# x loaded first on two queues, and the table set of Ln and Exp loaded by hand ahead of each norm's sum

## The reference

```python
def rms_norm(x, w):
    y = x * lax.rsqrt(jnp.mean(x * x, axis=-1, keepdims=True) + EPS)
    return y * w

for i in range(2):
    hn = rms_norm(h, norm_mix_pre[i])
    m = deltanet_stickbreak_mixer(hn, ...) if i == 0 else s5_mixer(hn, ...)
    h = h + rms_norm(m, norm_mix_post[i])
    hn = rms_norm(h, norm_ffn_pre[i])
    h = h + rms_norm(swiglu_ffn(hn, ...), norm_ffn_post[i])
```

## Time and profile before

| | us |
|---|---|
| median of 3 runs | 3101.07 (3097.99 to 3101.18) |
| profiled execution | 3102.59 |
| its span | 3100.8 |
| PE busy | 2824.9 (91%) |
| ACT busy | 684.9 (22%) |
| DVE busy | 1235.6 (40%) |
| GpSimd busy | 948.7 (31%) |

### The profile page before, as it was taken

The page is one execution under the profiler, slowest core; times in us unless marked ns, Lnnn a source line. Parts: engine busy times, 40 slices in busy tenths (PEclk is TensorE's granted clock), DMA queues, the critical chain, the costliest instruction groups (busy, mean ns, idle before and its releaser), DMA issues.

```text
span 3100.8 us, 44315 instructions
## 1 busy us (share of the span) xinstructions
PE 2824.9 (91%) x17789; PEld 2701.1 (87%) x17789; DVE 1235.6 (40%) x2076; ACT 684.9 (22%) x1168; POOL 948.7 (31%) x390
## 2 busy tenths in 40 slices
PE   3999979989999999999999876559999999999996
PEld 2999968877888999999999775459989999999995
DVE  2665137755424444444433421630152233222234
ACT  3222125545434000000001431220250000000012
POOL 3344400000043443443333322005243444443330
PEclk8999989999999999999999987679999999999998
DMA  4222441111122222222221235961122111111102
GB/s 136 70 89 96 109 90 38 42 49 42 45 80 76 70 94 70 70 76 76 70 86 63 87 67 138 212 161 55 47 96 78 48 50 51 41 50 44 41 28 73
DMA packets 171849, 232.67 MB, mean 75 GB/s; under 512 B 58464, under 2 KB 137312, under 8 KB 169440
## 3 DMA queue, kind: packets, MB, share of 16 engines
q1 hardware_dynamic: 66064, 133.42, 15.0%
q10 hardware_dynamic: 105680, 97.77, 10.2%
HBM read 171.12 MB, written 60.03 MB: 75 GB/s over the span
## 4 chain that ended last, share of the span: by engine, by line
issue 35%; PE 32%; POOL 13%; DVE 7%; DMA 7%; ACT 4%; ACTq 2%; SPq 1%; POOLq 0%; DVEq 0%
POOL w_hi L600 8%; PE psum L628 6%; PE psum L629 6%; PE psum L630 6%; POOL w_lo L604 4%; DMA stage<-wstream 4%; PE psum L686 3%; DVE area L1944 2%; PE psum L1036 2%; PE psum L1008 1%; PE psum L887 1%; PE psum L877 1%; DVE area L1866 1%; DVE area L1871 1%; DMA area<-s_u 1%
## 5 line engine op out<-in xcount | busy, mean ns | idle before, releaser
L628 PE MATMUL psum<-x_hi,w_hi 128*128 128x344 f32 (+2 forms) x3600 | 1165.9, 324 | 55.2 <-DVE x_lo L1889 26.9
L629 PE MATMUL psum<-x_lo,w_hi 128*128 128x344 f32 (+2 forms) x3600 | 1159.1, 322 | 0.0
L630 PE MATMUL psum<-x_hi,w_lo 128*128 128x344 f32 (+2 forms) x3600 | 1154.2, 321 | 0.0
L600 POOL TENSOR_TENSOR w_hi<-stage,const 128x1024 fp32r<-128x1024 f32 x193 | 470.2, 2436 | 2047.0 <-PE psum L630 2027.3
L628 PEld LDWEIGHTS psum<-x_hi,w_hi 128*128 128x128 f32 x3600 | 681.4, 189 | 63.3 <-DVE x_lo L1889 26.6
L629 PEld LDWEIGHTS psum<-x_lo,w_hi 128*128 128x128 f32 x3600 | 680.6, 189 | 1.9
L630 PEld LDWEIGHTS psum<-x_hi,w_lo 128*128 128x128 f32 x3600 | 681.4, 189 | 0.0
L604 POOL TENSOR_TENSOR w_lo<-stage,w_hi 128x1024 fp32r<-128x1024 f32 x193 | 482.7, 2501 | 15.1
L628 PE MATMUL psum<-act_hi,w_hi 128*128 128x344 f32 (+1 forms) x1056 | 347.4, 329 | 22.1 <-DVE area L2331 16.7
L630 PE MATMUL psum<-act_hi,w_lo 128*128 128x344 f32 (+1 forms) x1056 | 342.0, 324 | 0.0
L629 PE MATMUL psum<-act_lo,w_hi 128*128 128x344 f32 (+1 forms) x1056 | 341.0, 323 | 0.0
(11 more groups left out here) (214 smaller groups left out, 2293.5 us busy)
## 6 DMA issues: line engine op xcount, KB each, us to landing
stage<-wstream SPq DMA_DIRECT2D x193, 512.0 KB, 3.6
s_set<-area ACTq DMA_DIRECT2D x8, 1860.0 KB, 7.9
proj<-area ACTq DMA_DIRECT2D x28, 520.0 KB, 2.6
area<-proj ACTq DMA_DIRECT2D x36, 256.0 KB, 3.5
resid<-area ACTq DMA_DIRECT2D x6, 1376.0 KB, 6.0
area<-resid ACTq DMA_DIRECT2D x6, 1376.0 KB, 9.8
area<-proj ACTq DMA_DIRECT2D x12, 520.0 KB, 5.0
area<-xT ACTq DMA_DIRECT2D x4, 1376.0 KB, 8.1
```

Source lines behind the costliest of these rows:

```text
L600: pool.tensor_tensor(per_block(w_hi[:, slot, :]), per_block(stage[:, h, :]), all_ones, ALU.mult).then_inc(high_split, 1)
L628: mm(out[:, 0:n], w_hi[:, slot, wk], hi[:, xk, a:a + n], start=first, stop=False)
L629: mm(out[:, 0:n], w_hi[:, slot, wk], lo[:, xk, a:a + n], start=False, stop=False)
L630: return mm(out[:, 0:n], w_lo[:, slot, wk], hi[:, xk, a:a + n], start=False, stop=last)
```

## The change

Stage 0 gets a buffer for part 2 of x (`first_h`), a second set of buffers for squares and a second bank for the sum of part 1. ACT issues part 0 of x first of all; SP issues the first 256 columns of `const`, `small`, parts 1 and 2, then the rest of `const`, all ahead of the weights. The zero writes move behind the convolution loop. In stage 0 part 1's squares no longer wait for part 0's sum, and PE's second sum waits for nothing but them. DVE's memsets of `rows`, `ga` and `gb` move ahead of stage 0, and its order there becomes pre 0, pre 1, low 0, pre 2, low 1, low 2. Every `norm_root` begins with a load of the set `natural_log_exp_and_others`, ahead of its wait for the sum, and so does the gates' part.

```diff
@@ norm buffers @@
+        first_h = [nv["h"][0], nv["h"][1], carve(3 * T_ROWS, KT, 344)]
+        first_sq = [sq_halves, [carve(3 * T_ROWS + KT * 344, 4, 344), carve(A1 + 3 * KT * CW, 4, 344)], sq_halves]
+        first_sums = [bank[7], bank[6], bank[7]]
@@ SP @@
+            sp.dma_start(const[:, 0:2 * P], const_in[:, 0:2 * P]).then_inc(params_loaded, 16)
+            sp.dma_start(small[:], small_in).then_inc(params_loaded, 16)
+            for c in (1, 2):
+                a, n = CUTS[c]
+                sp.dma_start(first_h[c][:, :, 0:n], xT[:, :, a:a + n]).then_inc(first_loaded[c], 16)
+            sp.dma_start(const[:, 2 * P:N_CONST_USED], const_in[:, 2 * P:N_CONST_USED]).then_inc(zeros_written, 16)
@@ PE norm_sum @@
-                if r == 0 and c:
-                    pe.wait_ge(nm_normed, c)
+                if r == 0:
+                    if c == 2:
+                        pe.wait_ge(nm_normed, 1)
@@ ACT norm_square @@
-                if e:
+                if r == 0 and c == 2:
+                    act.wait_ge(nm_sum, 1)
+                elif r:
                     act.wait_ge(nm_sum, e)
@@ ACT norm_root @@
+                nc.scalar.preload_act_table_set("natural_log_exp_and_others")
                 act.wait_ge(nm_sum, e + 1)
@@ ACT opening @@
-            act.dma_start(small[:], small_in).then_inc(params_loaded, 16)
-            act.dma_start(const[:], const_in[:, 0:N_CONST_USED]).then_inc(params_loaded, 16)
+            norm_load(0, 0)
             act.wait_ge(eps_ready, 3)
-            zeros = carve(18300, FRONT)
-            for g in range(4):
-                act.dma_start(proj[4 * g:4 * g + 4, :, 0:FRONT].rearrange("m p t -> p m t"),
...
-            act.dma_start(s5_k.rearrange("c m g w -> c (m g) w")[:, :, CH * G_CH:LAGS * G_CH],
...
-            act.wait_ge(params_loaded, 32)
-            norm_load(0, 0)
-            norm_load(0, 1)
             norm_square(0, 0, 1)
+            norm_square(0, 1, 1)
             norm_root(0, 0, 1)
-            norm_square(0, 1, 1)
+            norm_square(0, 2, 1)
             norm_root(0, 1, 1)
             norm_high(0, 0)
-            norm_load(0, 2)
             norm_high(0, 1)
-            norm_square(0, 2, 1)
             norm_root(0, 2, 1)
             norm_high(0, 2)
...
+            nc.scalar.preload_act_table_set("natural_log_exp_and_others")
             act.wait_ge(nm_normed, 3)
             ch(A(gate_col[0:4, :], small[0:4, A_LOG:A_LOG + 1], ACT.Exp))
...
             with act.Fori(0, 3) as i:
                 conv_tiles(i)
+            zeros = carve(18300, FRONT)
+            for g in range(4):
+                act.dma_start(proj[4 * g:4 * g + 4, :, 0:FRONT].rearrange("m p t -> p m t"),
...
+            act.dma_start(s5_k.rearrange("c m g w -> c (m g) w")[:, :, CH * G_CH:LAGS * G_CH],
...
             act.wait_ge(s5["params"], 16)
...
-            act.wait_ge(zeros_written, 80)
+            act.wait_ge(zeros_written, 96)
@@ DVE opening @@
-            dve.wait_ge(params_loaded, 32)
-            for c in range(3):
-                norm_pre(0, c)
-                norm_low(0, c)
...
             ch(V.memset(rows, 0.0))
             ch(V.memset(ga, 0.0))
+            ch.sync()
+            V.memset(gb, 0.0).then_inc(gate_dve, 1)
+            dve.wait_ge(params_loaded, 32)
+            norm_pre(0, 0)
+            norm_pre(0, 1)
+            norm_low(0, 0)
+            norm_pre(0, 2)
+            norm_low(0, 1)
+            norm_low(0, 2)
...
+            dve.wait_ge(x_ready, 3)
             ch(V.memset(keep, 1.0))
...
-            V.memset(gb, 0.0).then_inc(gate_dve, 1)
             dve.wait_ge(gate_act, 1)
```

More of the change, by code:

```diff
@@ L449, in trunk @@
         norm_sums = bank[7]
+        first_h = [nv["h"][0], nv["h"][1], carve(3 * T_ROWS, KT, 344)]
+        halves_of = lambda x: [x[:, 4 * i:4 * i + 4] for i in range(2)]
+        sq_halves = halves_of(nv["sq"])
+        first_sq = [sq_halves, [carve(3 * T_ROWS + KT * 344, 4, 344), carve(A1 + 3 * KT * CW, 4, 344)], sq_halves]
+        first_sums = [bank[7], bank[6], bank[7]]
         DOWN_BANKS = 3
@@ L675, in norm_sum @@
                 e = norm_event(r, c, m)
-                if r == 0 and c:
-                    pe.wait_ge(nm_normed, c)
+                sums, sq = (first_sums[c], first_sq[c]) if r == 0 else (norm_sums, sq_halves)
+                if r == 0:
+                    if c == 2:
+                        pe.wait_ge(nm_normed, 1)
                 elif r == 4 and c:
@@ L685, in norm_sum @@
                         pe.wait_ge(nm_square, 2 * e + k // 4 + 1)
-                    last = mm(norm_sums[:, 0:n], ones, nv["sq"][:, k, 0:n], start=(k == 0), stop=(k == KT - 1))
+                    last = mm(sums[:, 0:n], ones, sq[k // 4][:, k % 4, 0:n], start=(k == 0), stop=(k == KT - 1))
                 last.then_inc(nm_sum, 1)
@@ L1189, in norm_square @@
                     ks = slice(4 * half, 4 * half + 4)
-                    A(nv["sq"][:, ks, 0:n], x[:, ks], ACT.Square).then_inc(nm_square, 1)
+                    A(sq[half][:, :, 0:n], x[:, ks], ACT.Square).then_inc(nm_square, 1)
             def norm_root(r, c, m):
@@ L1214, in norm_high @@
                 act.wait_ge(nm_normed, 3 * r + c + 1)
[L1215 to L1218 removed]
+                h = first_h[c] if r == 0 else nv["h"][c % 2]
+                A(x_hi[:, :, a:a + n], h[:, :, 0:n], ACT.Copy).then_inc(nm_high, 1)
+            norm_load(0, 0)
             act.wait_ge(eps_ready, 3)
[L1221 to L1229 removed]
             for _i in range(6):
@@ L1309, in _ @@
                 conv_tiles(i)
+            zeros = carve(18300, FRONT)
+            for g in range(4):
+                act.dma_start(proj[4 * g:4 * g + 4, :, 0:FRONT].rearrange("m p t -> p m t"),
+                              zeros.rearrange("p (a t) -> p a t", a=1).to_broadcast([P, 4, FRONT])
+                              ).then_inc(zeros_written, 16)
+            no_lag = (LAGS - CH) * G_CH
+            act.dma_start(s5_k.rearrange("c m g w -> c (m g) w")[:, :, CH * G_CH:LAGS * G_CH],
+                          zeros[0:G_CH, 0:no_lag].rearrange("p (a t) -> p a t", a=1).to_broadcast([G_CH, KT * GPT, no_lag])
+                          ).then_inc(zeros_written, 16)
             act.wait_ge(s5["params"], 16)
@@ L1888, in norm_low @@
                 dve.wait_ge(nm_high, 3 * r + c + 1)
-                V.tensor_tensor(x_lo[:, :, a:a + n], nv["h"][c % 2][:, :, 0:n], x_hi[:, :, a:a + n].bitcast(F32), sub
+                h = first_h[c] if r == 0 else nv["h"][c % 2]
+                V.tensor_tensor(x_lo[:, :, a:a + n], h[:, :, 0:n], x_hi[:, :, a:a + n].bitcast(F32), sub
                                 ).then_inc(x_ready, 1)
```

20 lines of the change are left out of this document (11 added, 9 removed).

## The result

The changed kernel takes 3050.71 us (3045.43 to 3054.22) against 3101.12 in the same comparison; the ratio is 0.9837, with a 95% interval from 0.9818 to 0.9855. That is 50.4 us less, where 43.4 were forecast; the time lies in the range of 3047 to 3067.

What follows compares the result with a forecast made beforehand. TensorE, busy 91% of a 3100.8 us span, bounds the kernel, so only its idle places can be won: 33 (opening) + 0.4 (convolutions) + 10 (norm loads) = 43.4, giving 3057.7 us, range 3047 to 3067.

Steps and rivals of the forecast that it cites:

- The load of x: Opening: first part of x lands at 11.5 (bounds 9.5 and 15.6), including some 3 us of start and receipt.
- The gates: Six gate groups at 2.8 us each, starting at 35.6; projection starts at 55.4 against 88.70, gain 33.
- The term of 2 us: Gates: 2 us added once for a low clock after PE idles, before the first two groups.
- The rival with the low clock: Zero writes cost 7.7 and PE is at 1.2 GHz after each opening pause, 2 + 3.7 dearer: 3063.4; chance 0.10.
- The chain behind the gates: From gates to first convolution: 4.4 us shorter relative to PE, by the early memset (3.1) and a dropped table load.
- The convolutions: Convolution stage: they bound PE; PE's time moves by the zero writes' price less 4.4, taken -0.4.
- Z: Price of the zero writes moved behind the last convolution tile: taken as 4, with 7.66 and 2.8 as alternatives.
- The hand-loaded set: Later norms: Exp's 1.28 us load saved where PE idles for the result; sum 10.0, bounds 7 and 14.
- The delta-net rows: Evidence that one set serves Ln and Exp: there Exp follows Ln with no load and no idle time.
- the rival that the hand load does nothing: Ln and Exp keep getting own loads; the 10 and some 3 in the opening are lost: 3070.7; chance 0.04.
- upper bound of 14, for two places: Later norms' gain is 14 if a shorter idle keeps the clock up at two of the places.
- Drain: Rival: every load costs the drain too, 2.66 us a switch; eight times 1.38 more, 3046.7; chance 0.03.

Runs made afterwards that it cites:

- e8: The changed kernel with all three parts of x on SP's queue, ACT's queue empty in the opening; 3054.83 us.
- e7: The changed kernel with DVE's memset of gb, and the signal letting ACT read the gates, back behind the other memsets; 3048.15 us.
- e10: e3 with GpSimd's second split operation cut to 64 of 1024 columns for 24 of the projection's 28 slabs, computation partly left out; 3037.61 us.
- e9: e5 plus four matmuls of constants between the gates and the projection; 3037.74 us, ratio 0.9800.
- e11: e3 plus four matmuls of constants ahead of the projection; 3039.23 us, ratio 0.9799.
- e1: The changed kernel without its hand-made table loads, the opening staying as changed; 3082.52 us, ratio 0.9923.
- e2: The kernel before with one edit, the table set loaded at the head of every norm root; 3078.28 us, ratio 0.9923.
- e5: The changed kernel with the gates in three products of 352, 344 and 344 columns in place of six of half that; 3050.39 us.
- e3: The changed kernel with matmuls of constants in PE's two idle times: 8 before the first gate group, 9 before the third; 3054.28 us.

## Why the prediction was right, and where it was not

The sign and the total held: 50.4 us by medians, 54.3 between the spans, for 43.4. That the total came so close is luck: the gain up to the projection was 7 us too high, and the convolutions and the later norms brought 9 and 8 more than forecast. Step by step:

**The load of x.** Forecast 11.5 for the first square, with bounds of 9.5 and 15.6; it came at 8.98, below the lower bound. The 3 us for start and receipt stand in no row and were too many. Nor did SP's traffic beside it cost what the sum took: in e8, with no other part of x beside it, the first part gained only 0.6. That the queues bring nothing held (e8); the reading of 214 GB/s as what one queue moves did not, since one queue moved 350 to 364 there. What the buffer for the third part, the second set of squares and DVE's new order brought each was not tried alone. PE's wait of 15.8 us for the third part's squares, ahead of the sum at 63.30 in the kernel before, is gone as well. GpSimd's splits started at 19.18 as forecast (19), and DVE's `x_lo` beside them took 3.90 and then 5.0 each, as taken (5.27).

**The gates.** This is the step that failed. The sum took six groups at 2.8 us and 2 us for a low clock, and had 19.8 us from the first gate matmul to the projection; it was 30.4, at 1.2 GHz but for the first 0.9. The term of 2 us came from a sum's products: seven of them ran at 0.50 in 4.1 us before the clock came back (this window is the second sum's, 344 columns, though the 7.16 set beside it is the first's; the second took 7.06). It was carried over to products of half the width, with which the clock did not come back. Mis-sized by some 11 us; with the gates' start 3.8 us early, that makes 26.4 of the forecast 33. The early start is in part the first square's 2.5, and `x_ready` 2 came at 41.7 and not at the 44 that was taken (44.9 by the walk's own durations). The rival with the low clock carried it as 2 more.

**The chain behind the gates.** ACT did follow PE through the gates and was through with Ln 4.3 us behind PE in place of 8.2, so 3.9 sooner, where 4.4 were forecast. But the DVE part of that chain (16.1 us from 66.66 to 82.71) was 3.3 longer than before, since some of its operations met GpSimd's split, and the lead over PE at the first convolution was 0.6 and not 4.4. e7 shows that the memset itself was worth nothing.

**The convolutions.** The forecast let PE's waits shrink by the lead less the zero writes' 4 us. In fact the stretch fell by 9.4: the chain went over from 1940 to 1620 ns an operation, left PE behind, and the zero writes then fell into slack. The forecast had treated DVE's times as fixed, though rows 5 had shown such an operation at 5.27 in place of 3.09 beside GpSimd. The mechanism is shown by e10 and by the meetings counted in all traces: six fewer, at 1.9 us each, make up the 11.5 us by which the 36 operations got shorter. That moving the two groups against each other changes the course is shown by e9 and e11. The change was not made for that, so this gain is luck. Why 8.21 us still gave the fast course and 8.81 the slow one was not tested, and that e1's fastest execution had the fast course is a guess from its time.

**The zero writes.** Z was 3.9 us, forecast 4.

**The hand-loaded set.** The waits for x_lo, and the last one of norm 4, shrank by the forecast 1.28. In norm 2 the sum had named the wrong wait as its first: the 2.50 at 1757.26 stayed, and the 2.17 at 1727.44 shrank by 1.23. The delta-net rows were the right witness, and the rival that the hand load does nothing is out (e2). The gain was 18 between these two traces (14 to 18 over the table), of which the sum gives 10. PE's idle time fell by some 12, and its busy time by some 6 for the same matmuls, which goes with the clock: at norm 3 it did not fall in a wait of 3.16 us, and the window of 4 us behind it holds 25 matmuls in place of 14. The prediction had this as its upper bound of 14, for two places. How the 6 us divide over places was not tested by itself.

**Drain.** The rule of the Trainium skill, "ScalarE: Activation LUTs", section "What ACT_TABLE_LOAD costs", of 2.66 us a switch is not borne out where it would count: with the load gone the four waits that shrank above fell by 1.27 to 1.29.

## What to carry to other kernels

Ask of each stretch that a change will make earlier what clock TensorE will have in it, and take the figure from rows with products of the same width: here idle times of up to 3.7 us around narrow products cost 10 us. A few filling matmuls avoided that, and whole cuts the larger part of it. Where two engines slow each other, a chain has no fixed length: its offset against the other engine belongs in the sum; here two microseconds of added work were worth fifteen. Count how many of its operations start while the other engine is at work, and at what price each. Load Ln's and Exp's common set once, ahead of the wait, wherever the two follow each other on a path.

## What the runs showed of the hardware that was not expected

Behind an idle time of 3.67 us, with matmuls of 172 and 176 columns one every 0.21 us, the granted clock fell within 0.9 us and stayed at 0.50 for the 29.5 us that they went on; those of 352 had it at 1.00 1.2 us into the projection and 6 us into the gates in e5. With both idle times filled the narrow groups stayed at 1.00 (e3), as they had in the kernel before. The Trainium skill, "TensorE: Matmul & The Clock Gate", section "Part 1: The HAM clock gate", tells of sustained matmul activity as what releases the clock; here PE was busy in nearly every microsecond of the gates and it was not released. Busy is what the profile models: at the same low clock a matmul of 352 columns took 0.29 us and one of 176 took 0.21, so the narrow ones moved fewer columns in a busy microsecond. No run parts this from the number of weight loads.

DVE's 128x1040 scalar_tensor_tensor took 1.30 us, or 3.18 to 3.44 when it started while GpSimd was at a 1024-column operation; nothing in between was seen in 468 of them. Over 36 operations that makes means of 1301 ns with half of GpSimd's splitting left out, and 1567 to 1670 or 1939 to 2104 beside all of it, by the number of such starts.
